# Three edits to the prologue of an encoder kernel: unread matmuls on TensorE in two places, and one weight split moved on VectorE

## What is computed

```python
mod = jax.nn.silu(c) @ mod_w[l] + mod_b[l]
sh1, sc1, g1, sh2, sc2, g2, sh3, sc3, g3 = jnp.split(mod, N_MOD, axis=-1)
h = modulate(rms_norm(x, norm_g[l, 0]), sh1, sc1)          # h * (1 + sc1) + sh1
x = x + 0.5 * g1[:, None, :] * swiglu(h, ffn1_w1[l], ffn1_w3[l], ffn1_w2[l])
```

## Time and profile before

| | us |
|---|---|
| median of three runs | 2078.43 |
| lowest and highest of them | 2076.39, 2078.64 |
| the profiled execution, its own time | 2080.41 |
| its span | 2078.6 |
| TensorE matmul busy | 2009.0 (97%) |
| VectorE busy | 1326.2 (64%) |
| ScalarE busy | 690.7 (33%) |
| GpSimd busy | 89.9 (4%) |

### The profile page before, as it was taken

How to read it: one execution, slowest core, us unless ns; L and a number is a source line. 1 busy time by engine, 2 the same in 40 slices (tenths; PEclk the granted TensorE clock), 3 DMA queues, 4 the chain that set the end, 5 groups by cost and what they waited for, 6 DMA issues and landing times.

```text
span 2078.6 us, 24984 instructions
## 1 busy us (share of the span) xinstructions
PE 2009.0 (97%) x9410; PEld 1611.4 (78%) x9410; DVE 1326.2 (64%) x2143; ACT 690.7 (33%) x1061; POOL 89.9 (4%) x123
## 2 busy tenths in 40 slices
PE   7999999999899999999999999998989999999998
PEld 5878888777577788888878888886766787888886
DVE  6887876576884753643468787656779566455334
ACT  4432322332453431222342322224244443222223
POOL 0000000300100000000000000040000000000000
PEclk8999999999799999999999999999997999999999
DMA  8666743342112445433248485415420136353332
GB/s 294 198 196 214 233 120 94 97 113 72 46 31 61 138 156 162 154 93 99 82 130 258 147 257 151 122 55 138 107 66 11 41 102 194 101 192 112 101 94 79
DMA packets 398480, 265.81 MB, mean 128 GB/s; under 512 B 58032, under 2 KB 374168, under 8 KB 398360
## 3 DMA queue, kind: packets, MB, share of 16 engines
q1 hardware_dynamic: 397920, 263.83, 42.7%
q10 hardware_dynamic: 440, 0.38, 0.1%
HBM read 257.35 MB, written 6.82 MB: 127 GB/s over the span
## 4 chain that ended last, share of the span: by engine, by line
PE 65%; issue 21%; DVE 8%; ACT 3%; DMA 1%; SPq 1%; POOL 0%; DVEq 0%; POOLq 0%; ACTq 0%
PE ps L1815 19%; PE ps L1816 18%; PE ps L1817 18%; PE ps L2135 2%; PE ps L2154 1%; DVE w_lo L1071 1%; DMA stage<-in_ffn_w 1%; ACT w_hi L740 1%; DVE mod_acc L1092 1%; PE ps L2162 1%; PE ps L2145 1%; PE ps L2227 1%; DVE h_lo L1152 1%; PE ps L2232 1%; PE ps L2115 1%
## 5 line engine op out<-in xcount | busy, mean ns | idle before, releaser
L1815 PE MATMUL ps<-h_hi,w_hi 128*128 128x512 f32 x1725 | 682.4, 396 | 8.4 <-DVE w_lo L1071 5.7
L1816 PE MATMUL ps<-h_lo,w_hi 128*128 128x512 f32 x1725 | 674.3, 391 | 0.0
L1817 PE MATMUL ps<-h_hi,w_lo 128*128 128x512 f32 x1725 | 674.0, 391 | 0.0
L1071 DVE TENSOR_TENSOR w_lo<-stage,w_hi 128x1024 fp32r<-128x1024 f32 (+2 forms) x322 | 375.6, 1190 | 128.7 <-ACT w_hi L740 126.7
L1815 PEld LDWEIGHTS ps<-h_hi,w_hi 128*128 128x128 f32 x1725 | 325.1, 188 | 87.3 <-issue 13.5
L740 ACT ACTIVATE w_hi<-stage 128x1024 fp32r<-128x1024 f32 (+2 forms) x322 | 318.3, 1017 | 197.2 <-PE ps L1817 177.1
L1817 PEld LDWEIGHTS ps<-h_hi,w_lo 128*128 128x128 f32 x1725 | 325.2, 189 | 69.2
L1816 PEld LDWEIGHTS ps<-h_lo,w_hi 128*128 128x128 f32 x1725 | 325.4, 189 | 65.4 <-issue 0.5
L1815 PE MATMUL ps<-g_hi,w_hi 128*128 128x512 f32 x704 | 283.0, 402 | 9.8 <-DVE x L1212 7.8
L1817 PE MATMUL ps<-g_hi,w_lo 128*128 128x512 f32 x704 | 280.4, 398 | 0.0
L1816 PE MATMUL ps<-g_lo,w_hi 128*128 128x512 f32 x704 | 280.4, 398 | 0.0
(11 more groups left out here) (333 smaller groups left out, 1633.1 us busy)
## 6 DMA issues: line engine op xcount, KB each, us to landing
stage<-in_ffn_w SPq DMA_DIRECT2D x210, 512.0 KB, 4.6
mod_stage<-in_mod_w SPq DMA_DIRECT2D x144, 512.0 KB, 5.4
stage<-in_ffn_w SPq DMA_DIRECT2D x64, 448.0 KB, 4.0
stage<-in_w_in SPq DMA_DIRECT2D x20, 512.0 KB, 3.9
mod_first<-in_mod_w SPq DMA_DIRECT2D x16, 512.0 KB, 9.4
stage<-in_w_out SPq DMA_DIRECT2D x16, 512.0 KB, 4.1
x_in<-in_x SPq DMA_DIRECT2D x4, 512.0 KB, 5.3
stage<-in_w_in SPq DMA_DIRECT2D x8, 256.0 KB, 4.5
```

The costliest lines, as they stand in the source:

```text
L1071: V.tensor_tensor(w_lo[:, c % RING, 0:n], stage[:, c % RING, 0:n], w_hi[:, c % RING, 0:n].bitcast(F32), ALU.subtract).then_inc(w_split_lo. ...
L1815: mm(out, hi, rhs_hi, start=first, stop=False)
L1816: mm(out, hi, rhs_lo, start=False, stop=False)
L1817: return mm(out, lo, rhs_hi, start=False, stop=last)
```

## The change

On TensorE, two float32 matmuls of the identity by columns 0 and 1 of `x` (512 columns each) stand ahead of the broadcast, and six fp32r matmuls of 512 columns on weight chunk 0 stand behind the sums of the scale. Both write bank 4 of PSUM, and nothing reads what they write. On VectorE the low part of weight chunk 1 moves from ahead of `first_mod(1)` to behind `norm_column`.

```diff
-            for c in range(AHEAD):
-                split_lo(0, c)
+            split_lo(0, 0)
             first_mod(1)
             dve.wait_ge(*mod_done.at(0, -2))
             norm_column(0, 0)
+            split_lo(0, 1)
             for n in range(KT):
                 scaled_lo(0, 0, n)
...
+            for n in range(2):
+                pe.wait_ge(*x_new.at(0, n - KT))
+                mm(ps[:, 4, :], ident[:], x[:, n, :], start=True, stop=True)
             rms_bcast(0, 0)
             first_sum(1)
+            pe.wait_ge(*w_split_hi.at(0, 0))
+            for n in range(6):
+                mm(ps[:, 4, :], w_hi[:, 0, 0:P], w_hi[:, 0, 0:SW], start=True, stop=True)
```

## The result

The changed kernel takes 2081.93 us, the kernel before 2078.43 (medians of 17 runs each); the ratio is 1.0018, with a 95% interval of 1.0011 to 1.0024. That is 3.5 us slower, between 2.3 and 5.0 us by the interval. I had forecast 2078.3 and a range up to 2080.4.

What follows compares the result with a forecast made beforehand. The prediction took VectorE's chain to bound the prologue at 44.6 us; added matmuls cost 0, and gains became waits except -0.1 us, giving 2078.3 us against 2078.43, range 2075.9 to 2080.4.

Steps and rivals of the forecast that it cites:

- What bounds the prologue: Up to 44.6 us, VectorE's gapless chain including the shift piece landings sets the time, by 0.4 us over TensorE.
- The unread matmuls cost nothing where they stand: Ahead of the broadcast and behind the sums, both groups fit into TensorE's waits: cost 0, at most 0.1 us each.
- The gain turns into waits: Up to 1.2 us won on VectorE becomes a DMA wait; TensorE's 0.42 us wait at line 1887 becomes some 1.8 us.
- the 1.7 us of faster products: Tile 0's first eight matmuls take 0.22 instead of 0.43 us each; the 1.7 us is given back at line 1887.
- what follows is moved as a block: -0.1 us: From line 1887 TensorE goes on at 44.53 instead of 44.63, and everything behind it moves by -0.1 us.
- rival C: The longer wait at line 1887 lets the clock fall, costing 1.5 us: 2080.0; chance 0.15.
- the 2.2 us of those rows: Earlier wait, followed at 134.1 us by 3.3 us at half clock; taken as the length that decides.
- The size of C: Behind line 1887, dense matmuls at half rate over 3.3 us lose 1.65 us, less 0.1: 1.5 us.
- nothing in the change touches a load: Argued against the second shift piece landing a us earlier, which would give 2077.2; chance 0.15.
- The range: Whole kernel: 2075.9 to 2080.4 us, letting a median of a few runs be off by a us.
- Rival A: Prologue: all 13.4 us at half clock are TensorE work on the path; wins back 6.7 us, 2071.7; chance 0.03.

Runs made afterwards that it cites:

- e10: Changed kernel plus 64 semaphore increments in TensorE's first two idle stretches; 2.6 us above the kernel before, ratio 1.0012.
- e6: Kernel before plus only the six unread fp32r matmuls behind the sums of the scale; 2080.45 us, ratio 1.0005.
- e3: Kernel before with only the VectorE split of weight chunk 1 moved; 2078.74 us, ratio 0.9997.
- e7: Kernel before with the shift accumulator's interleaved sums 1.4 us of products earlier in tile 1, nothing added; 2083.73 us, ratio 1.0023.
- e8: Kernel before plus 24 semaphore increments on TensorE ahead of its first wait; 2082.21 us, ratio 1.0015.
- e1: Changed kernel plus six more unread fp32r matmuls directly ahead of the wait at line 1887; 2081.73 us, ratio 1.0012.
- e2: Changed kernel with the shift accumulator's interleaved sums 1.4 us of products later in tile 1; 2081.17 us, ratio 1.0009.
- e4: Kernel before plus both groups of unread matmuls, VectorE split not moved; 2080.72 us, ratio 1.0011.
- e9: Changed kernel plus six unread matmuls at line 1887's wait and 64 semaphore increments in TensorE's first two idle stretches; 2078.66 us, ratio 1.0000.
- e11: Changed kernel with later sums in tile 1, tile 2's shift column at k = 5 and 60 semaphore increments; 2080.34 us, ratio 1.0008.

## Why the prediction was wrong

- **What bounds the prologue: right.** VectorE and the landings set 44.4 us; the second shift piece started at 30.20 (forecast 30.3 to 30.4) and line 1887 at 44.38 (44.53).
- **The unread matmuls cost nothing where they stand: right.** Four records took 1.88 us (2.0 forecast), the six ended as tile 0's first product was due, and the broadcast was released by GpSimd.
- **The gain turns into waits: right.** The wait at line 1887 was 1.46 us (1.8 forecast), and the 1.7 us of faster products were given back.
- **The sum, "what follows is moved as a block: -0.1 us": wrong, and this is the step that failed.** TensorE did go on 0.25 us earlier, but what followed was not moved as a block: it was 2.9 us late by 54 us, and lost again in the waits at 391 and 1407 us. First, rival C happened. I had its place and its mechanism, but ruled it down with "It decides once the wait at line 1887 reaches the 2.2 us of those rows; mine is shorter by 0.4". The clock fell behind a wait of 1.46 us, and of 1.33 in e10; it held behind 1.43 in e6 and 1.1 in e3. One pair of rows was no threshold. At the very wait of these rows, 2.0 us long ahead of the record at 133.6 us, the clock held in six other traces, the changed kernel's among them.
- **The size of C was too small by half.** I took 3.3 us at half clock and 1.65 us lost from the earlier trace rows, where plain products follow the wait. Here the low stretch lasted 6.6 us (10 in e7), and the cost by matching the traces was 3.15 us. Why it lasted longer is not shown: the interleaved sums follow here, but at 394 us in before plain products ran at half clock for 6 us too.
- **Missing altogether: the instruction count.** The forecast priced added instructions by TensorE's time alone and said that nothing in the change touches a load. It touched TensorE's instruction loads, one of which moved from behind TensorE's wait at 390 us into SyncE's eight issues, in both layers. e8 has this without any added matmul and an excess of 2.9 us (1.2 to 5.0). The traces account for less. The waits of line 1212 grew from 7.8 us to 9.9 in the changed kernel and 10.7 in e8, but much of it comes back, as the clock is low behind that wait in any case: in before it is low from 393.5 us for 6.8 us and TensorE starts at 394.12; in the changed kernel it is low from 394.3 us for 6.8 us and TensorE starts at 396.14, so that less of its work meets the low clock. At the end of the execution the two places have cost 0.6 us in the changed kernel, 1.2 in e1, 0.7 in e2, 0.8 in e4 and 1.8 in e8, against -0.6 to 0.2 us in e6, e9 and e11, which have no such overlap. What the rest of e8's excess is stays open.
- **The range.** It left 0.4 us above rival C's 2080.0, although the text lets a median be off by a us. With that us it would have ended at 2081.0, still below the 2081.93 measured.
- **Rival A, and with it the rule of the Trainium skill, "TensorE: Matmul & The Clock Gate", section "Terms"**, by which a low clock costs its length times one minus K/N: the low stretch of the prologue went from 13.4 to 6.6 us and the time rose, so the trace does not bear the rule out there. For the stretch behind line 1887, where TensorE is the bound, 6.6 us times a half is 3.3, and 3.15 was measured. In these two stretches the rule comes out where TensorE's work is what is waited for, and not where it is not.

What stays open: the two costs taken alone (2.6 and 3.0 us) sum to more than the change's 3.5 us, which the intervals allow and no run explains. By matching, the fall is worth 3.1 us and the two places 0.6 to 1.8 us, so the fall is the larger part in the traces, while the medians of e1 and e8 say that the loads alone bring as much. Each kernel has one trace, so how often its clock falls at line 1887, and whether added instructions also change how often it falls further back, is not known. Why an issue of SyncE is held up while an instruction load of TensorE is under way was not tried. That it is so was seen in all five kernels with such an overlap traced here, counting the changed one, in both layers.

## What to carry to other kernels

Keeping TensorE's clock up only pays where TensorE is what is waited for; where another engine sets the end, faster products merely make a later wait longer, and a wait of 1.3 to 1.9 us can let the clock fall for 3 to 10 us of work that is then on the path. Before making an engine faster ahead of a wait, move work into that wait, and check the next wait behind it too. Adding instructions to an engine can shift its instruction loads for the rest of the program: after a small edit, compare where they fall with the load issues of other engines, and test an unexplained loss with a handful of increments in an idle stretch.

## What was not expected of the hardware

- A handful of instructions with no work in them, 24 semaphore increments in an idle stretch at the start, lengthened two of TensorE's waits, at 389 us and 1404 us, by 2.9 us in sum; the median rose by as much. Thirteen added instructions left the load at 397 us, and about 23 moved it to 386 us, across TensorE's wait from 390 to 394 us. Why it jumps there is not shown.
- Behind one and the same wait the clock falls in some executions and not in others. Ahead of the record at 133.6 us (before's time) TensorE waits 2.0 us in eleven of the twelve traces; the clock fell behind it in five of them (before, e1, e2, e6, e7), which costs 1.55 us by matching. Behind a wait of 1.6 us at 440 us it fell in eight of twelve, for 1.6 us. A single trace therefore cannot say how long a wait may be, and a kernel's time differs by some us from one execution to the next with nothing changed: e3's profiled execution, which lacks both falls and has a shorter one at 392 us, ended 4.3 us before that of the kernel before. The 17 runs of before span 5.5 us.
- One load issue of line 606 on SyncE takes 0.43 us, and 1.0 to 1.75 us for one of them while an instruction load of 16384 bytes is under way.
- Transposes of float32 blocks run at 421 ns a record up to 14.3 us and at 273 ns from 14.5 us on, although the clock is shown at 1.00 all that time. The trace's first record of the clock is a step to 1.00 at 14.57 us, just where they get faster after a dense run. So I take it that the clock was low before, and that the 1.00 shown ahead of that record is not a measurement; no run here tests it. The rows before, of line 1961 up to 14.4 us and from 14.6 us:

```profile
L1961 PE MATMUL ps<-ident,x_in x21: 408/421/476, 9.6 to 14.3; 128*128 128x128 f32 x21
```

```profile
L1961 PE MATMUL ps<-ident,x_in x9: 272/273/408, 14.3 to 15.3; 128*128 128x128 f32 x9
```
